# Expert stage of a hybrid attention and mixture-of-experts step: one tile per loop turn, three places for weight blocks, exact tile count

## Chip, core and metric

The kernel runs on one core of a Trainium2 chip. The metric is the device time of one execution in microseconds, as the median of several runs. TensorE (PE), VectorE (DVE), ScalarE (ACT), GpSimd (POOL) and SyncE (SP) each work through a list of their own; they wait for each other through semaphores. DMA transfers are issued by SP and by POOL, each on a queue of its own.

## What is computed

One layer of a backbone on 640 tokens (512 latent, 128 context), width 1024: a combined projection, two kinds of attention, a merge, and then a mixture of experts with 16 experts, of which each token uses two. The change touches only that last part:

```python
def hier_moe(h, w_coarse, b_coarse, w_fine, b_fine, w_gate_up, w_down):
    ...                                    # group of experts, then the top 2 of its 4 experts
    for e in range(N_EXPERTS):             # 16; D = 1024, EXPERT_FF = 512
        gg, uu = jnp.split(t @ w_gate_up[e], 2, axis=-1)
        out = out + combine[:, e:e + 1] * ((jax.nn.silu(gg) * uu) @ w_down[e])
```

All of it is float32. The kernel gets float32 accuracy on TensorE by splitting both operands into a rounded part ("hi") and a rest ("lo") and by making three matmuls, hi·hi, hi·lo and lo·hi.

## The kernel before

The 1280 pairs of token and expert are sorted by expert in memory (`expert_rows`) into tiles of 128 rows. Each expert has one tile, and an expert with more than 128 rows has further tiles. A tile is one matrix of 128 rows by 1024 that is multiplied with the weights of one expert.

Per tile the expert stage does this:

- POOL loads the tile's rows into `expert_in` (line 1848, `load_rows`, 512 KB). `expert_in` has two places, `s` = 0 and 1.
- TensorE transposes them (line 1618, `turn_x`), ACT rounds them (882, `round_x`), DVE takes the rest (1337, `rest_x`).
- SP loads the three weight blocks of the expert, gate, up and down, each 2 MB as four chunks of 512 KB (line 660), alternately into `w_raw` and `w_raw_odd`. ACT rounds each chunk to `w_hi` (878), DVE takes the rest to `w_lo` (1332). There are two places of each; a block reuses the place of the block two before it.
- TensorE makes the gate and the up half of the hidden rows (lines 1632 to 1634, `gate_up`, 48 matmuls). ACT and DVE apply the activation (887, 1344, 1349). TensorE transposes the result (1655, `turn_hidden`), ACT and DVE split it (896, 1353), and TensorE makes the output rows (1647 to 1649, `down`, 24 matmuls).
- ACT copies the output to `expert_out_rows` (892, `take_out`; two places), and POOL stores it back to `expert_rows` (1853, `store_rows`, 512 KB) and waits until it has landed.

The order is written out by hand and software-pipelined by one tile. TensorE's turn for a tile is: `gate_up(tile)`, `turn_x(tile + 1)`, `down(tile - 1)`, `turn_hidden(tile)`. The loop body holds two tiles (`for s in range(2)`), and the number of loop turns comes at run time from `control`, which the routing on DVE has written; `route_done` tells the other engines that it is there. So the stage handles an even number of tiles. POOL's turn for one tile is:

```python
load_rows(2 * i + 3 + s, 1 - s)     # waits x_turned >= tile - 1 + OFF, then the DMA
store_rows(2 * i + s, s, i)         # waits for take_out, DMA, waits until it has landed
```

With `t` as the tile that is stored, the load ahead of it is that of tile `t + 3`. Before the loop POOL has loaded the tiles 0, 1 and 2.

Ahead of the stage SP loads the first gate block into `w_raw` and the first up block into `w_raw_odd`, whose memory is that of the last normalization step; so the second one waits for `yb_done` and for the stores of the normalized rows. The other blocks wait for `route_done`, as which expert they are of is read from `control`. Behind the stage POOL gathers the two output rows of each token (1872), and DVE, ACT and POOL combine and normalize them.

Of the kernel before, what the change touches and what calls it, by code (L numbers as in the profile page):

```python
# [60 lines left out]
TILES = NE + OVER + (NE + OVER) % 2  # L61
# [34 lines left out]
def hybrid_step(nc, t):  # L96

    with ExitStack() as ctx:
# [296 lines left out]
        s4 = ExitStack()  # L395
        ot_hi = [sb("oA_turned_hi", [P, KD, NT * P], F32R, s4)]
# [39 lines left out]
        raw_odd = sb("w_raw_odd", [P, NC_CH, 2, CW], F32, s4)  # L436
# [26 lines left out]
        xs = sb("expert_in", [P, 2, D], F32, s6)  # L463
        xt_hi = sb("expert_in_hi", [P, 2, KD, P], F32R, s6)
        xt_lo = sb("expert_in_lo", [P, 2, KD, P], F32R, s6)
# [4 lines left out]
        yo = sb("expert_out_rows", [P, 2, D], F32, s6)  # L470
# [16 lines left out]
        xs_in = [sem(f"expert_in{i}") for i in range(2)]  # L487
# [4 lines left out]
        raw2_in = [sem(f"w_raw_odd_in{c}") for c in range(NC_CH)]  # L492
# [7 lines left out]
        y_st = [sem(f"expert_out_stored{i}") for i in range(2)]  # L500
# [19 lines left out]
        def landing(q, half, c):  # L520

            if q % 2:
                return raw_odd[:, c], raw2_in[c], 16 * (half + 1)
            return w_raw[:, c], raw_in[c], 16 * (NB + half + 1)
# [5 lines left out]
        def step_blocks(i, s):  # L530

            return [(6 * i + n, n % 2, 3 * i + n // 2) for n in range(3 * s + 2, 3 * s + 5)]
# [7 lines left out]
        def last_pair_of_tiles(eng):  # L540

            return eng.value_load(ctl[0:1, 0:1], min_val=NE // 2 - 1, max_val=TILES // 2 - 1)
# [51 lines left out]
        def _(sp):  # L594
# [61 lines left out]
            def block_in(q, par, half, chunk, r):  # L656
                for c in range(NC_CH):
                    dst, done, _ = landing(par, half, c)
                    sp.wait_ge(lo_done, NC_CH * (NB + q - 2) + c + 1)
                    sp.dma_start(dst, chunk(r, c)).then_inc(done, 16)  # L660

# [10 lines left out]
            def tile_expert(tile):  # L672
                e = sp.value_load(ctl[0:1, bass.ds(1 + tile, 1)], min_val=0, max_val=NE - 1)
                return lambda r, c: expert_chunk(bass.ds(e, 1), r, c).rearrange("p o k n -> p (o k) n")

            sp.wait_ge(route_done, 1)
            last_pair = last_pair_of_tiles(sp)
            with sp.Fori(0, last_pair) as i:
                for s in range(2):
                    chunk = tile_expert(2 * i + 1 + s)  # L680
                    for r, (q, par, half) in enumerate(step_blocks(i, s)):
                        if r == 2:
                            chunk = tile_expert(2 * i + s)
                        block_in(q, par, half, chunk, r)
            chunk = tile_expert(2 * last_pair + 1)
            for r, (q, par, half) in enumerate(step_blocks(last_pair, 0)):
                block_in(q, par, half, tile_expert(2 * last_pair) if r == 2 else chunk, r)
            block_in(6 * last_pair + 5, 1, 3 * last_pair + 2, chunk, 2)
# [20 lines left out]
        def _(act):  # L709
# [159 lines left out]
            act.wait_ge(pj_ready, N_PJ2)  # L869

            def split_hi_moe(block):
                q, par, half = block
                for c in range(NC_CH):
                    src, done, value = landing(par, half, c)
                    act.wait_ge(done, value)
                    if not (isinstance(q, int) and q < 2):
                        act.wait_ge(moe_used, used(q - 2) + c + 1)
                    act.copy(w_hi[:, (NB + par) % 2, c], src).then_inc(hi_done, 1)  # L878

            def round_x(tile, s):  # L880
                act.wait_ge(x_turned, tile + 1 + OFF)
                act.copy(xt_hi[:, s].rearrange("p k q -> p (k q)"), pair[1][:]).then_inc(xh_done, 1)
# [16 lines left out]
            def act_tile(i, s, final):  # L899
                tile, (gate, up, down) = 2 * i + 1 + s, step_blocks(i, s)  # L900
                split_hi_moe(down)
                gate_tanh(tile, gate[0])
                nq = 6 * i + 3 * s + 5
                if final:
                    split_hi_moe((nq, 1, 3 * i + 2))
                else:
                    split_hi_moe((nq, (3 * s + 5) % 2, 3 * i + (3 * s + 5) // 2))
                    round_x(tile + 1, s)
                    split_hi_moe((nq + 1, (3 * s + 6) % 2, 3 * i + (3 * s + 6) // 2))
                take_out(tile - 1, s, down[0])  # L910
                round_hidden(tile)

# [3 lines left out]
            last_pair = last_pair_of_tiles(act)  # L916
            act.wait_ge(y_free, OFF)
            round_x(0, 0)
            split_hi_moe((2, 0, 1))
            gate_tanh(0, 0)  # L920
            split_hi_moe((3, 1, 1))
            round_x(1, 1)
            round_hidden(0)
            with act.Fori(0, last_pair) as i:
                for s in range(2):
                    act_tile(i, s, False)
            act_tile(last_pair, 0, True)
            take_out(2 * last_pair + 1, 1, 6 * last_pair + 5)

# [5 lines left out]
        def _(dve):  # L935
# [373 lines left out]
            for i in range(2):  # L1309
# [4 lines left out]
            link(dve.tensor_tensor(cle[:, 0, 0:MORE // 2], ovc[:, NE - 1:NE].to_broadcast([P, MORE // 2]),  # L1314
                                   tab[:, T_PAIR:T_PAIR + MORE // 2], ALU.is_gt))
            link(dve.tensor_reduce(cf[:, 0:1], cle[:, 0, 0:MORE // 2], AX.X, ALU.add))
            link(dve.tensor_scalar(cf[:, 0:1], cf[:, 0:1], float(NE // 2 - 1), None, ALU.add))
# [10 lines left out]
            def split_lo_moe(block):  # L1328
                q, par, _ = block
                for c in range(NC_CH):  # L1330
                    dve.wait_ge(hi_done, NC_CH * (NB + q) + c + 1)
                    dve.tensor_tensor(w_lo[:, (NB + par) % 2, c], landing(par, 0, c)[0], w_hi[:, (NB + par) % 2, c].bitcast(F32),  # L1332
                                      ALU.subtract).then_inc(lo_done, 1)

            def rest_x(tile, s):
                dve.wait_ge(xh_done, tile + 1 + OFF)
                dve.tensor_tensor(xt_lo[:, s].rearrange("p k q -> p (k q)"), pair[1][:],  # L1337
                                  xt_hi[:, s].rearrange("p k q -> p (k q)").bitcast(F32), ALU.subtract).then_inc(xl_done, 1)
# [18 lines left out]
            def dve_tile(i, s, final):  # L1357
                tile, (gate, up, down) = 2 * i + 1 + s, step_blocks(i, s)
                split_lo_moe(down)
                silu(tile)  # L1360
                nq = 6 * i + 3 * s + 5
                if final:
                    split_lo_moe((nq, 1, 0))
                    times_up(tile, up[0])
                else:
                    split_lo_moe((nq, (3 * s + 5) % 2, 0))
                    times_up(tile, up[0])
                    rest_x(tile + 1, s)
                    split_lo_moe((nq + 1, (3 * s + 6) % 2, 0))
                rest_hidden(tile)  # L1370

            dve.wait_ge(route_done, 1)
            last_pair = last_pair_of_tiles(dve)
            split_lo_moe((0, 0, 0))
            split_lo_moe((1, 1, 0))
            rest_x(0, 0)
            split_lo_moe((2, 0, 0))
            silu(0)
            split_lo_moe((3, 1, 0))
            times_up(0, 1)  # L1380
            rest_x(1, 1)
            rest_hidden(0)
            with dve.Fori(0, last_pair) as i:
                for s in range(2):
                    dve_tile(i, s, False)
            dve_tile(last_pair, 0, True)
# [13 lines left out]
        def _(pe):  # L1400
# [214 lines left out]
            def turn_x(tile, s, landed):  # L1615
                pe.wait_ge(xs_in[s], landed)
                for k in range(KD):
                    last = pe.transpose(pair[1][:, k * P:(k + 1) * P], xs[:, s, k * P:(k + 1) * P], ident[:])
                last.then_inc(x_turned, 1)

            def gate_up(tile, s, blks):
                for r, (q, par, _) in enumerate(blks):
                    if r == 0:
                        pe.wait_ge(xl_done, tile + 1 + OFF)
                        pe.wait_ge(hid_done, tile + OFF)
# [46 lines left out]
            with pe.Fori(0, last_pair) as i:  # L1672
                for s in range(2):
                    pe_tile(i, s, False)
# [269 lines left out]
```

## Time and profile before

| | us |
|---|---|
| median of 3 runs (lowest, highest) | 1662.11 (1661.32, 1665.05) |
| span of the profiled execution | 1662.6 |
| TensorE busy | 1336.0 (80%) |
| TensorE weight load busy | 1087.6 (65%) |
| VectorE busy | 1085.6 (65%) |
| ScalarE busy | 705.8 (42%) |
| GpSimd busy | 250.3 (15%) |
| mean granted TensorE clock | 0.910 |

The whole span falls into projections, attention, merge and normalization, routing (to about 1164 us), the scatter of the rows (to 1190 us), the expert stage (1195 to 1581 us) and the final combination. Shares over the whole span hide that; the expert stage is read by itself, from its own windows.

### The profile page before, as it was taken

The numbers are of one execution on the slowest core, as the hardware profiler recorded it, in microseconds if no ns is written. First come the engines' busy times: TensorE is split into PE (matmuls) and PEld (weight loads), VectorE is DVE, ScalarE is ACT, GpSimd is POOL, SyncE is SP. The second block draws the span as 40 slices with busy tenths as digits, with TensorE's granted clock in tenths as the row PEclk, the third lists the DMA queues.
The fourth block names the chain that finished last, engine by engine and source line by source line (L and its number), as shares of the span: only waits on it lengthen the run. The fifth ranks groups of instructions, "written<-read, shape, count | busy, mean of one in ns | idle before, by whom it ended". The sixth has DMA issues, their size and how long they took to land.

```text
span 1662.6 us, 21046 instructions
## 1 busy us (share of the span) xinstructions
PE 1336.0 (80%) x6852; PEld 1087.6 (65%) x6852; DVE 1085.6 (65%) x1891; ACT 705.8 (42%) x1008; POOL 250.3 (15%) x278
## 2 busy tenths in 40 slices
PE   2599999967999877889995999783299999999800
PEld 0377776655788766788884788563178887777600
DVE  6556552489822377755556634766289999999665
ACT  3523333232322366545444212002078787778600
POOL 0002111011120000000000331453300000000044
PEclk7799999989999999999997999985599999999955
DMA  6545555433473576611203884421889999999642
GB/s 229 167 139 191 193 181 182 147 116 100 146 236 110 151 176 154 180 41 59 73 17 104 298 297 134 166 89 63 316 291 393 392 392 393 392 392 392 258 177 88
DMA packets 152376, 333.05 MB, mean 200 GB/s; under 512 B 17595, under 2 KB 23259, under 8 KB 152299
## 3 DMA queue, kind: packets, MB, share of 16 engines
q1 hardware_dynamic: 123914, 233.22, 41.3%
q0 software_dynamic: 26944, 93.59, 16.1%
q10 hardware_dynamic: 1440, 5.24, 1.0%
q8 instruction: 45, 0.74, 0.2%
q14 instruction: 33, 0.26, 0.1%
HBM read 263.41 MB, written 68.58 MB: 200 GB/s over the span
## 4 chain that ended last, share of the span: by engine, by line
PE 50%; DVE 20%; DMA 13%; issue 9%; ACT 6%; POOL 1%; SPq 0%; ACTq 0%; POOLq 0%; DVEq 0%
PE psum_pair L1425 7%; PE psum_pair L1427 7%; PE psum_pair L1426 7%; DMA w_raw_odd<-in_w_gate_up 4%; DMA w_raw<-in_w_gate_up 4%; PE psum_pair L1518 4%; PE psum_pair L1505 3%; PE psum_pair L1557 3%; PE psum_pair L1558 3%; PE psum_pair L1559 3%; PE psum_pair L1495 3%; DVE w_lo L941 3%; DVE w_lo L1332 2%; ACT p_turned L375 2%; DVE minus_max L1101 2%
## 5 line engine op out<-in xcount | busy, mean ns | idle before, releaser
L941 DVE TENSOR_TENSOR w_lo<-w_raw,w_hi 128x1024 fp32r<-128x1024 f32 x124 | 146.5, 1222 | 152.0 <-ACT w_hi L715 150.2
L1425 PE MATMUL psum_pair<-w_hi,h_hi 128*128 128x512 f32 x520 | 212.3, 408 | 34.7 <-DVE w_lo L941 31.2
L1426 PE MATMUL psum_pair<-w_lo,h_hi 128*128 128x512 f32 x520 | 208.1, 400 | 0.0
L1427 PE MATMUL psum_pair<-w_hi,h_lo 128*128 128x512 f32 x520 | 208.1, 400 | 0.0
L1101 DVE TENSOR_REDUCE minus_max<-psum_pair 128x1 f32<-128x640 f32 (+1 forms) x160 | 114.3, 715 | 96.6 <-PE psum_pair L1495 96.0
L715 ACT CAST w_hi<-w_raw 128x1024 fp32r<-128x1024 f32 x124 | 124.2, 1048 | 120.8 <-DMA w_raw<-in_w_ada 61.5
L799 ACT ACTIVATE p_unnormed<-psum_pair,minus_max 128x640 f32<-128x640 f32 (+1 forms) x160 | 113.4, 709 | 142.2 <-DVE minus_max L1101 142.2
L1332 DVE TENSOR_TENSOR w_lo<-w_raw,w_hi 128x1024 fp32r<-128x1024 f32 x120 | 143.2, 1222 | 22.8 <-ACT w_hi L878 18.6
L1332 DVE TENSOR_TENSOR w_lo<-w_raw_odd,w_hi 128x1024 fp32r<-128x1024 f32 x120 | 143.1, 1221 | 12.0 <-ACT w_hi L878 8.4
L878 ACT CAST w_hi<-w_raw 128x1024 fp32r<-128x1024 f32 x120 | 123.4, 1051 | 45.4 <-DMA w_raw<-in_w_gate_up 26.2
L1425 PEld LDWEIGHTS psum_pair<-w_hi,h_hi 128*128 128x128 f32 x520 | 101.2, 195 | 63.4 <-issue 39.3
L878 ACT CAST w_hi<-w_raw_odd 128x1024 fp32r<-128x1024 f32 x120 | 123.7, 1050 | 35.2 <-DMA w_raw_odd<-in_w_gate_up 25.3
L1632 PE MATMUL psum_pair<-w_hi,expert_in_hi 128*128 128x512 f32 x320 | 129.9, 406 | 7.3 <-DVE expert_in_lo L1337 7.2
L1495 PE MATMUL psum_pair<-k_bundle,q_bundle 128*128 128x512 f32 (+1 forms) x576 | 126.3, 337 | 6.8 <-ACT p_unnormed L799 6.1
L1518 PE MATMUL psum_pair<-v_bundle,p_turned 128*128 128x64 f32 (+1 forms) x1008 | 131.4, 275 | 0.0
L1634 PE MATMUL psum_pair<-w_hi,expert_in_lo 128*128 128x512 f32 x320 | 128.0, 400 | 0.0
L1633 PE MATMUL psum_pair<-w_lo,expert_in_hi 128*128 128x512 f32 x320 | 128.0, 400 | 0.0
L1518 PEld LDWEIGHTS psum_pair<-v_bundle,p_turned 128*128 128x128 f32 x1008 | 122.9, 193 | 1.3
L1427 PEld LDWEIGHTS psum_pair<-w_hi,h_lo 128*128 128x128 f32 x520 | 100.9, 194 | 22.1
L1426 PEld LDWEIGHTS psum_pair<-w_lo,h_hi 128*128 128x128 f32 x520 | 101.4, 195 | 20.4
L1495 PEld LDWEIGHTS psum_pair<-k_bundle,q_bundle 128*128 128x128 f32 x576 | 87.2, 191 | 14.6 <-issue 7.9
L726 ACT ACTIVATE turned_staging<-psum_pair 128x1024 f32<-128x1024 f32 (+1 forms) x38 | 36.3, 957 | 105.2 <-PE psum_pair L1453 105.2
(267 smaller groups left out, 2424.7 us busy)
## 6 DMA issues: line engine op xcount, KB each, us to landing
w_raw<-in_w_gate_up SPq DMA_DIRECT2D x80, 512.0 KB, 8.9
w_raw_odd<-in_w_gate_up SPq DMA_DIRECT2D x80, 512.0 KB, 9.4
w_raw<-in_w_in SPq DMA_DIRECT2D x52, 512.0 KB, 5.2
w_raw<-in_w_ada SPq DMA_DIRECT2D x48, 512.0 KB, 5.4
w_raw<-in_w_down SPq DMA_DIRECT2D x40, 512.0 KB, 9.5
w_raw_odd<-in_w_down SPq DMA_DIRECT2D x40, 512.0 KB, 9.5
expert_rows<-zeros POOLq DMA_DIRECT2D x27, 512.0 KB, 6.0
k_bundle<-k_transposed SPq DMA_DIRECT2D x28, 384.0 KB, 8.7
```

The costliest lines, as they stand in the source:

```text
L878: act.copy(w_hi[:, (NB + par) % 2, c], src).then_inc(hi_done, 1)
L941: dve.tensor_tensor(w_lo[:, b % 2, c], w_raw[:, c], w_hi[:, b % 2, c].bitcast(F32), ALU.subtract).then_inc(lo_done, 1)
L1101: dve.tensor_reduce(nmax[:, m % RR:m % RR + 1], spair(m)[:, 0:width(j)], AX.X, ALU.max, negate=True).then_inc(nb_done, 1)
L1332: dve.tensor_tensor(w_lo[:, (NB + par) % 2, c], landing(par, 0, c)[0], w_hi[:, (NB + par) % 2, c].bitcast(F32), ALU.subtract).then_inc(lo_ ...
L1425: pe.matmul(bank(n), a_hi, hi, start=first, stop=False)
L1426: pe.matmul(bank(n), a_hi, lo, start=False, stop=False)
L1427: last = pe.matmul(bank(n), a_lo, hi, start=False, stop=end)
L1495: last = pe.matmul(spair(m)[:, c0:c0 + w], q, k[:, g, k0:k0 + w], start=g == 0, stop=g == 1)
L1518: last = pe.matmul(obank(j)[:, 0:w], ptb[:, j % 2, k], vb[bi % 2][:, vt, 0:w], start=k == 0, stop=k == len(tiles) - 1)
L1632: pe.matmul(out, xt_hi[:, s, kk], hi, start=kk == 0, stop=False)
L1633: pe.matmul(out, xt_hi[:, s, kk], lo, start=False, stop=False)
L1634: last = pe.matmul(out, xt_lo[:, s, kk], hi, start=False, stop=kk == KD - 1)
```

## The change

The expert stage is rewritten with a loop body of one tile.

- `TILES` is 25 and not 26, and `control[0]` holds the exact number of tiles less two, not a number of pairs. Two small DVE operations ahead of `route_done` go.
- The weight blocks get three places. Raw: `w_raw`, `w_raw_b`, `w_raw_c`. Split: the two places of `w_hi` and `w_lo` and a third, `w_hi_c` and `w_lo_c`. A block waits for the one three before it, on SP and on ACT. The two new raw places share memory with the turned attention rows, which are free after the last matmul of the output projection; SP loads the first up block and the second gate block there as soon as that matmul is done, without waiting for the normalization.
- `expert_in`, its split forms and `expert_out_rows` have one place where they had two. `load_rows` waits for the transposes of the tile just before it; `take_out` waits until the store of the tile before has landed.
- POOL's turn is: load of tile `t + 2`, store of tile `t`. TensorE's order within a tile stays.

```diff
-TILES = NE + OVER + (NE + OVER) % 2
+TILES = NE + OVER
...
-            sp.wait_ge(yb_done, NT)
-            sp.wait_ge(x1_st[0], 16 * 3)
-            sp.wait_ge(x1_st[1], 16 * 2)
             for c in range(NC_CH):
-                sp.dma_start(raw_odd[:, c], expert_chunk(0, 1, c)).then_inc(raw2_in[c], 16)
+                sp.dma_start(raw_b[:, c], expert_chunk(0, 1, c)).then_inc(raw_b_in[c], 16)
+            for c in range(NC_CH):
+                sp.dma_start(raw_c[:, c], expert_chunk(1, 0, c)).then_inc(raw_c_in[c], 16)
...
+                for c in range(NC_CH):
+                    sp.wait_ge(lo_done, NC_CH * (NB + q - 3) + c + 1)
...
-            def take_out(tile, s, q):
+            def take_out(tile, q):
                 act.wait_ge(moe_used, used(q + 1))
-                act.wait_ge(y_free, tile - 1 + OFF)
-                act.copy(yo[:, s], pair[3][:]).then_inc(y_copied, 1)
+                act.wait_ge(y_free, tile + OFF)
+                act.copy(yo[:], pair[3][:]).then_inc(y_copied, 1)
...
-            def load_rows(tile, s):
-                pool.wait_ge(x_turned, tile - 1 + OFF)
-                pool.dma_start(xs[:, s], slot_tiles[bass.ds(tile, 1)]...).then_inc(xs_in[s], 16)
+            def load_rows(tile):
+                pool.wait_ge(x_turned, tile + OFF)
+                pool.dma_start(xs[:], slot_tiles[bass.ds(tile, 1)]...).then_inc(xs_in, 16)
...
-            def store_rows(tile, s, half):
+            def store_rows(tile):
                 pool.wait_ge(y_copied, tile + 1 + OFF)
-                pool.dma_start(slot_tiles[...], yo[:, s]).then_inc(y_st[s], 16)
-                pool.wait_ge(y_st[s], 16 * (half + 1))
+                pool.dma_start(slot_tiles[...], yo[:]).then_inc(y_st, 16)
+                pool.wait_ge(y_st, 16 * (tile + 1))
                 pool.nop().then_inc(y_free, 1)
...
-            load_rows(2, 0)
-            with pool.Fori(0, last_pair) as i:
-                for s in range(2):
-                    load_rows(2 * i + 3 + s, 1 - s)
-                    store_rows(2 * i + s, s, i)
+            pool.wait_ge(x_turned, 1 + OFF)
+            pool.dma_start(xs[:], slot_tiles[1]).then_inc(xs_in, 16)
+            with pool.Fori(0, middle) as i:
+                load_rows(i + 2)
+                store_rows(i)
```

TensorE's loop after the change:

```python
with pe.Fori(0, middle) as i:
    half_of_hidden(i + 1, gate_block(i + 1), 0)
    half_of_hidden(i + 1, up_block(i + 1), 1)
    turn_x(i + 2)
    down(i, down_block(i))
    turn_hidden(i + 1)
```

## Rows read from the trace of the kernel before

**Rows 1.** Stretches of the stage: busy time by engine, PEclk, DMA share, GB/s
```profile
1240.00:1250.00 10.00, 10.00 (x49) 8.24 (x48) 9.32 (x10) 8.39 (x10) 0.70 (x2) 1.00 0.99 354
...
1300.00:1540.00 240.00, 236.36 (x1089) 191.42 (x1089) 219.81 (x206) 189.87 (x205) 13.85 (x26) 1.00 1.05 392
```

**Rows 2.** TensorE in order of time: start us, us, line, what, count
```profile
1230.30 1.03 PE L1618 MATMUL psum_pair<-identity,expert_in 128*128 128x128 f32 x8
...
1236.75 0.60 PE L1655 MATMUL psum_pair<-identity,expert_hidden 128*128 128x128 f32 x4
...
1248.34 1.04 PE L1618 MATMUL psum_pair<-identity,expert_in 128*128 128x128 f32 x8
...
1356.93 1.03 PE L1618 MATMUL psum_pair<-identity,expert_in 128*128 128x128 f32 x8
...
1543.66 1.04 PE L1618 MATMUL psum_pair<-identity,expert_in 128*128 128x128 f32 x8
```

**Rows 3.** Chain of waits within the stage: start us, us, what ended last
```profile
1374.62 10.40 DMA w_raw<-in_w_gate_up
```

**Rows 4.** Instructions on `expert_rows`: count, ns min/median/max, first and last start
```profile
L1853 POOL DMA_DIRECT2D expert_rows<-expert_out_rows x20: 532/537/539, 1239.6 to 1578.4; - x20
```

**Rows 5.** GpSimd in order of time: its stores and loads, idle time and releaser
```profile
1239.63 0.54 POOL L1853 DMA_DIRECT2D expert_rows<-expert_out_rows  x1 [24.44 <-ACT expert_out_rows L892]
1247.72 0.53 POOL L1848 DMA_DIRECT2D expert_in<-expert_rows  x1 [7.55 <-DMA expert_rows<-expert_out_rows]
...
1350.05 0.54 POOL L1853 DMA_DIRECT2D expert_rows<-expert_out_rows  x1 [10.51 <-ACT expert_out_rows L892]
...
1357.50 0.53 POOL L1848 DMA_DIRECT2D expert_in<-expert_rows  x1 [6.91 <-DMA expert_rows<-expert_out_rows]
```

**Rows 6.** ScalarE in order of time: copy of the first tile's output
```profile
1237.90 1.01 ACT L892 COPY expert_out_rows<-psum_pair 128x1024 f32<-128x1024 f32 x1
```

**Rows 7.** TensorE in order of time: last matmul of the stage
```profile
1576.20 0.40 PE L1649 MATMUL psum_pair<-w_hi,hidden_lo 128*128 128x512 f32 x1
```

**Rows 8.** Chain of waits at the end of the stage
```profile
1576.71 1.02 ACT expert_out_rows L892
...
1578.38 2.88 DMA expert_rows<-expert_out_rows
```

**Rows 9.** DMA issues of 1200 to 1540 us: count, KB each, median us to landing
```profile
expert_in<-expert_rows POOLq DMA_DIRECT2D x17, 512.0 KB, 6.6
expert_rows<-expert_out_rows POOLq DMA_DIRECT2D x17, 512.0 KB, 6.6
```

**Rows 10.** DMA issues, 1238 to 1241 us
```profile
w_raw<-in_w_gate_up SPq DMA_DIRECT2D x2, 512.0 KB, 7.0
expert_rows<-expert_out_rows POOLq DMA_DIRECT2D x1, 512.0 KB, 7.3
```

**Rows 11.** SyncE in order of time: weight loads issued, start us, us
```profile
1235.84 3.95 SPq L660 DMA_DIRECT2D w_raw<-in_w_gate_up  x4
1241.77 4.03 SPq L660 DMA_DIRECT2D w_raw_odd<-in_w_gate_up  x4
1247.17 4.22 SPq L660 DMA_DIRECT2D w_raw<-in_w_down  x4
```

**Rows 12.** TensorE in order of time: its one stall inside the stage
```profile
1216.16 0.65 PE L1655 MATMUL psum_pair<-identity,expert_hidden 128*128 128x128 f32 x4 [2.18 <-DVE expert_hidden L1349]
1217.49 0.49 PE L1632 MATMUL psum_pair<-w_hi,expert_in_hi 128*128 128x512 f32 x1 [0.68 <-DVE expert_in_lo L1337]
```

**Rows 13.** Stretches of 1 us after that stall, columns as in the first group
```profile
1218.00:1219.00 1.00, 1.00 (x5) 0.78 (x5) 0.17 (x1) 0.00 (x0) 0.00 (x0) 0.78 1.09 408
1219.00:1220.00 1.00, 1.00 (x4) 0.81 (x3) 0.00 (x0) 0.44 (x1) 0.00 (x0) 0.50 1.03 414
...
1222.00:1223.00 1.00, 1.00 (x6) 0.83 (x5) 0.00 (x0) 0.88 (x1) 0.00 (x0) 1.00 0.08 31
```

**Rows 14.** Stretch of 1 us between the scatter's end and the stage
```profile
1191.00:1192.00 1.00, 0.00 (x0) 0.00 (x0) 0.00 (x0) 0.00 (x0) 1.00 (x3) 0.50 0.07 27
```

More of the change, by code:

```diff
@@ L486, in hybrid_step @@
         scat_st = sem("rows_scattered")
-        xs_in = [sem(f"expert_in{i}") for i in range(2)]
+        xs_in = sem("expert_in")
         x_turned = sem("expert_in_turned")
@@ L514, in hybrid_step, with landing, landed, expert_hi @@
         w_dn = t["w_down"][0].rearrange("e (k p) n -> p e k n", p=P)
[L520 to L524, printed above, removed]
+        def landing(place, c):
+            return ((w_raw, raw_in, NB), (raw_b, raw_b_in, 0), (raw_c, raw_c_in, 0))[place][0][:, c]
+        def landed(place, turn, c):
+            done, earlier = ((raw_in, NB), (raw_b_in, 0), (raw_c_in, 0))[place]
+            return done[c], 16 * (earlier + turn + 1)
+        def expert_hi(place, c):
+            return hi_c[:, c] if place == 2 else w_hi[:, 1 - place, c]
+        def expert_lo(place, c):
+            return lo_c[:, c] if place == 2 else w_lo[:, 1 - place, c]
         def used(q):
             return NC_CH * q + OFF
-        def step_blocks(i, s):
-            return [(6 * i + n, n % 2, 3 * i + n // 2) for n in range(3 * s + 2, 3 * s + 5)]
+        def gate_block(tile):
+            return 3 * tile - 1, 2, tile - 1
+        def up_block(tile):
+            return 3 * tile, 0, tile
+        def down_block(tile):
+            return 3 * tile + 4, 1, tile + 1
+        def last_block(tile):
+            return 3 * tile + 2, 2, tile
         def expert_chunk(e, r, c):
@@ L654, in _ @@
                 load_x(tt)
[L656 to L660, printed above, removed]
             for c in range(NC_CH):
@@ L665, in _, with expert_in @@
             sp.wait_ge(pj_ready, last_no[NB - 1] + 1)
[L666 to L668 removed]
             for c in range(NC_CH):
[L670 to L672 removed]
+                sp.dma_start(raw_b[:, c], expert_chunk(0, 1, c)).then_inc(raw_b_in[c], 16)
+            for c in range(NC_CH):
+                sp.dma_start(raw_c[:, c], expert_chunk(1, 0, c)).then_inc(raw_c_in[c], 16)
+            def expert_in(block, tile, r):
+                q, place, _ = block
                 e = sp.value_load(ctl[0:1, bass.ds(1 + tile, 1)], min_val=0, max_val=NE - 1)
[L674 removed]
+                for c in range(NC_CH):
+                    sp.wait_ge(lo_done, NC_CH * (NB + q - 3) + c + 1)
+                    sp.dma_start(landing(place, c), expert_chunk(bass.ds(e, 1), r, c).rearrange("p o k n -> p (o k) n")).then_inc(
+                        landed(place, 0, c)[0], 16)
             sp.wait_ge(route_done, 1)
[L677 to L688 removed]
+            middle = middle_tiles(sp)
+            with sp.Fori(0, middle) as i:
+                expert_in(up_block(i + 1), i + 1, 1)
+                expert_in(down_block(i), i, 2)
+                expert_in(gate_block(i + 2), i + 2, 0)
+            expert_in(up_block(middle + 1), middle + 1, 1)
+            expert_in(down_block(middle), middle, 2)
+            expert_in(last_block(middle + 1), middle + 1, 2)
             sp.wait_ge(moe_over, 1)
@@ L868, in _, with round_x @@
                 act.nop().then_inc(sm, OFF)
-            act.wait_ge(pj_ready, N_PJ2)
             def split_hi_moe(block):
-                q, par, half = block
+                q, place, turn = block
                 for c in range(NC_CH):
[L874 to L880, printed above, removed]
+                    act.wait_ge(*landed(place, turn, c))
+                    if not (isinstance(q, int) and q < 3):
+                        act.wait_ge(moe_used, used(q - 3) + c + 1)
+                    act.copy(expert_hi(place, c), landing(place, c)).then_inc(hi_done, 1)
+            def round_x(tile):
                 act.wait_ge(x_turned, tile + 1 + OFF)
-                act.copy(xt_hi[:, s].rearrange("p k q -> p (k q)"), pair[1][:]).then_inc(xh_done, 1)
+                act.copy(xt_hi[:].rearrange("p k q -> p (k q)"), pair[1][:]).then_inc(xh_done, 1)
             def gate_tanh(tile, q):
@@ L897, in round_hidden @@
                                scale=0.5).then_inc(ah_done, 1)
[L899 to L911, printed above, removed]
+            act.wait_ge(pj_ready, last_no[NB - 1] + 1)
             split_hi_moe((0, 0, 0))
@@ L1355, in rest_hidden @@
                                          ALU.mult, ALU.subtract).then_inc(al_done, 1)
[L1357 to L1370, printed above, removed]
             dve.wait_ge(route_done, 1)
-            last_pair = last_pair_of_tiles(dve)
+            middle = middle_tiles(dve)
             split_lo_moe((0, 0, 0))
             split_lo_moe((1, 1, 0))
-            rest_x(0, 0)
-            split_lo_moe((2, 0, 0))
+            split_lo_moe(gate_block(1))
+            rest_x(0)
             silu(0)
-            split_lo_moe((3, 1, 0))
+            split_lo_moe(up_block(1))
             times_up(0, 1)
-            rest_x(1, 1)
+            rest_x(1)
             rest_hidden(0)
[L1383 to L1386, printed above, removed]
+            with dve.Fori(0, middle) as i:
+                split_lo_moe(down_block(i))
+                silu(i + 1)
+                split_lo_moe(gate_block(i + 2))
+                times_up(i + 1, up_block(i + 1)[0])
+                rest_x(i + 2)
+                split_lo_moe(up_block(i + 2))
+                rest_hidden(i + 1)
+            split_lo_moe(down_block(middle))
+            silu(middle + 1)
+            split_lo_moe(last_block(middle + 1))
+            times_up(middle + 1, up_block(middle + 1)[0])
+            rest_hidden(middle + 1)
             dve.wait_ge(s7_in, 64)
@@ L1613, in _, with turn_x @@
                 pe.nop().then_inc(sm, OFF)
-            def turn_x(tile, s, landed):
-                pe.wait_ge(xs_in[s], landed)
+            def turn_x(tile):
+                pe.wait_ge(xs_in, 16 * (tile + 1))
                 for k in range(KD):
-                    last = pe.transpose(pair[1][:, k * P:(k + 1) * P], xs[:, s, k * P:(k + 1) * P], ident[:])
+                    last = pe.transpose(pair[1][:, k * P:(k + 1) * P], xs[:, k * P:(k + 1) * P], ident[:])
                 last.then_inc(x_turned, 1)
[L1621 to L1625, printed above, removed]
-                    out = pair[0][:, r * FF:(r + 1) * FF]
-                    for c in range(NC_CH):
-                        pe.wait_ge(lo_done, NC_CH * (NB + q) + c + 1)
-                        for k in range(2):
-                            kk = 2 * c + k
-                            hi, lo = w_hi[:, (NB + par) % 2, c, k], w_lo[:, (NB + par) % 2, c, k]
-                            pe.matmul(out, xt_hi[:, s, kk], hi, start=kk == 0, stop=False)
-                            pe.matmul(out, xt_hi[:, s, kk], lo, start=False, stop=False)
-                            last = pe.matmul(out, xt_lo[:, s, kk], hi, start=False, stop=kk == KD - 1)
-                        last.then_inc(moe_used, 1)
@@ L1637, in down, with half_of_hidden @@
-            def down(tile, blk):
-                q, par, _ = blk
+            def half_of_hidden(tile, block, r):
+                q, place, _ = block
+                if r == 0:
+                    pe.wait_ge(xl_done, tile + 1 + OFF)
+                    pe.wait_ge(hid_done, tile + OFF)
+                out = pair[0][:, r * FF:(r + 1) * FF]
+                for c in range(NC_CH):
+                    pe.wait_ge(lo_done, NC_CH * (NB + q) + c + 1)
+                    for k in range(2):
+                        kk = 2 * c + k
+                        hi, lo = expert_hi(place, c)[:, k], expert_lo(place, c)[:, k]
+                        pe.matmul(out, xt_hi[:, kk], hi, start=kk == 0, stop=False)
+                        pe.matmul(out, xt_hi[:, kk], lo, start=False, stop=False)
+                        last = pe.matmul(out, xt_lo[:, kk], hi, start=False, stop=kk == KD - 1)
+                    last.then_inc(moe_used, 1)
@@ L1639, in down @@
+            def down(tile, block):
+                q, place, _ = block
                 pe.wait_ge(al_done, tile + 1 + OFF)
```

115 lines of the change are left out of this document (59 added, 56 removed).

## Prediction, written before the change was run

> **What bounds the kernel now.** I read the expert stage by itself. First the busy time by stretch: from 1300 to 1540 us all 16 DMA engines are full (share 1.05, 392 GB/s) and TensorE is busy for 236.4 of 240 us [rows 1]. Then TensorE in order of time, where the start of `turn_x` marks a tile. I call that start T. Between 1230.30 and 1356.93 us lie 7 tiles, 18.09 us each; between 1356.93 and 1543.66 lie 10, 18.67 us each [rows 2]. A tile moves twelve weight chunks, one load of rows and one store, 14 x 0.524 MB = 7.34 MB, and 7.34 MB at 392 GB/s takes 18.7 us. TensorE alone takes 6.45 us from T to `turn_hidden` (1230.30 to 1236.75) and 11.6 us from there to the next T (1236.75 to 1248.34), in all 18.0 us. So the stage is first bound by TensorE, later by DMA bandwidth with TensorE 0.6 us behind; the chain of waits shows it as a 10.40 us transfer into `w_raw` [rows 3]. The third thing to read is GpSimd's turn: store, wait until it has landed, load [rows 5]. It is on no path to the end now, since it works one tile further ahead than TensorE needs.
>
> **The change, part by part.**
>
> *Exact tile count.* The output was stored 20 times [rows 4], so 20 tiles ran. That is 16 + 3 or 16 + 4 rounded up. The trace cannot say which; the routing of the given inputs, worked out from the reference, has three experts with more than 128 rows (144, 140 and 191) and the next has 126. So 19 tiles are real, and one tile of 18.7 us goes. The two small DVE operations are worth nothing that can be seen.
>
> *Three places for weights.* Loads and splits run one block further ahead. In the part bound by bandwidth this buys nothing per tile, since the bytes of a tile stay. If nothing else binds, it extends the stretch of 18.1 us tiles by a few.
>
> *One place for rows in and out.* Here a loop closes. TensorE's transposes of tile t + 2 need `load_rows(t + 2)`. That comes on GpSimd behind `store_rows(t - 1)` having landed, which needs `take_out(t - 1)`, which needs `down(t - 1)`, and this stands on TensorE behind the transposes of tile t + 1. Before, the load behind the same store was that of tile t + 3, with a whole tile in hand. Behind the stalled transposes TensorE has queued `down`, `turn_hidden` and the next 48 matmuls, so the stall is the stage's. From T to the next T:
> - T to the end of `down`. `turn_hidden` starts at T + 6.45 [rows 2]; at the end of the stage the copy starts 0.51 us after the last matmul's start [rows 7, 8], and that start is 0.23 us ahead of `turn_hidden`. So the copy can start at T + 6.73. In the trace it starts at T + 7.60 (1237.90) [rows 6], held by splits that wait for a place of `w_hi`; with three places they don't.
> - The copy's start to the store's issue: 1237.90 to 1239.63, 1.73 us [rows 5, 6]. Store issued at T + 8.46.
> - Store issued to load issued: 1239.63 to 1247.72, 8.09 us, later 1350.05 to 1357.50, 7.45 us [rows 5]. I take 7.8.
> - Load issued to landed: median 6.6 us [rows 9]; 0.1 us for the start of the transposes is my estimate.
> Sum 8.46 + 7.8 + 6.6 + 0.1 = 22.9 us, 4.3 us more than the 18.67 of now. The two transfers take 6.6 to 7.3 us beside weight traffic [rows 9, 10] and 2.88 us on empty channels [rows 8]. With a period of 22.9 us the channels would carry 320 GB/s. The stretch 1240 to 1250 had 354 GB/s [rows 1], weight chunks issued from 1235.84, 1241.77 and 1247.17 [rows 11], and its store still took 7.3 us [rows 10] and its load was issued T + 17.4. This is nearly the pattern that I expect: chunks from about T + 5, T + 11 and T + 16. So I take the loaded times; the empty ones (8.46 + 3.8 + 2.9 + 0.1 = 15.3, under 18.67, no stall at all) are the lower end.
>
> What the Trainium skill says speaks against this. "DMA: Bandwidth & Descriptors" (Queues, rings and completion order) has each DMA engine go round-robin between queues, packet by packet. With two queues at work a 512 KB transfer would then get half the rate, by my estimate some 4.3 us, and the loop would take 8.5 + 5.2 + 4.3 + 0.1 = 18.1 us: no stall. The trace disagrees wherever both queues work: 6.6 to 7.3 us.
>
> *The clock.* TensorE idled 2.18 and 0.68 us around 1217 us [rows 12]. After that its granted clock was 0.5, the 1.2 GHz level, and back at 1.0 by 1222 [rows 13]. The 48 matmuls from 1217.49 to T at 1230.30 took 12.8 us, where they otherwise take 11.3: a price of 1.5 us. A stall of 4 us in each tile should bring the same fall, and part of it lies on the loop, on transposes and `down`. Bounds 0 and 1.5 us per tile; I take 0.7, as a later store also meets fewer weight chunks. Period 23.6 us, from the second tile of the loop on.
>
> *Start.* The first up and the second gate block load earlier, and a third block now loads during the scatter. That can leave a backlog when the first rows are loaded, where the channels are now empty (share 0.07 [rows 14]): between 0 and 6.6 - 2.9 = 3.7 us later. I take 1.5, for the scatter uses another queue.
>
> *End.* From T of the last tile (1543.66) to the last store's landing (1578.38 + 2.88 = 1581.26) it is 37.6 us [rows 2, 8]. Weights no longer wait there, but the slow clock costs 1.5: I take 38.5. The part behind the stage stays.
>
> **The sum.** T of the third tile moves from 1230.30 to 1231.8. Sixteen further tiles follow: 22.9 + 15 x 23.6 = 376.9 us, so T of the last tile is 1608.7, and the last store has landed at 1647.2, against 1581.3: 65.9 us more (17 intervals of 18.4 us, 313.4 us, become 16 intervals of 23.6). The profiled span of 1662.6 becomes 1728.5; it lies 0.5 us above the median, so the forecast is 1728 us.
>
> **Rivals.**
> - *The loop of the rows doesn't bind: faster.* If the two transfers together take under 10 us, the period stays at 18.7. They can by finding the channels free (2.88 us each), or by an even share with the weights: 2 x 0.524 MB / 392 GB/s = 2.7 us, with the 1.5 us beyond pure transfer in the 2.88, is 4.2 us each. Then the tile saved decides: T of the last tile 1230.3 + 16 x 18.7 = 1529.5, last store 1567, 14 us less: about 1648 us; with some tiles at 18.1, 1642. It decides below a period of 19.4 us, where 16 intervals fit into 313 us. For it: the idle channels that a slower loop itself makes. The rule of the Trainium skill cited above would bring this case about. Against it: 7.3 us in the least loaded comparable stretch [rows 10]. Chance 0.12.
> - *The loop binds, but mildly.* The slower loop frees the channels for one of the two transfers, 3 to 4 us instead of 6.6, and the period is 20 to 21.5. At 20.5: 1231.8 + 328 + 38.5 = 1598.3, or 17 us more, 1679 us. Slower as well. For it: at 23 us per tile a fifth of the DMA time is idle. Chance 0.15.
> - *The tile isn't saved.* If the chip's routing gave 20 tiles, one further period comes on top: 1728 + 24 = 1752 us. Against it: 126 against 128 rows is exact counting. Chance 0.02.
> - *No change,* within 0.2%, which is about what a measurement of this kernel can tell: the first rival with a period of 19.2 to 19.6. Chance 0.03.
> - The forecast, a period of 21.5 to 25 us: 0.68.
>
> **Range.** The lower end is a period of about 20.5 us, 1679, rounded to 1678. The upper end is all the clock's price and 7.3 us transfers: period 25 and a start 3.7 us later, T of the last tile 1234.0 + 22.9 + 15 x 25 = 1631.9, last store 1670.4, 89 us more: 1751. Left out are the faster cases and half of the tail above. Faster 0.12, same 0.03, slower 0.85.
>
> **What the changed kernel's profile would show.** 19 stores to `expert_rows`; intervals between the first transposes of two tiles of 22 to 25 us; nearly every tile's transposes waiting for the DMA into `expert_in`, 3 to 5 us; under GpSimd the load released by the landing of the store each time; GB/s at 300 to 340 in place of 392 through the stage; a granted clock that falls in most tiles; ScalarE no longer waiting for weight DMAs. I would be wrong if the transfers on GpSimd's queue took 3 to 4 us beside the weights, so that the transposes never waited and the interval stayed under 19 us.

## The result and the profile after

| | before | after |
|---|---|---|
| median, us | 1663.58 (4 runs) | 1738.99 (4 runs, 1731.09 to 1742.6) |
| ratio to before | | 1.0441 (95%: 1.0423 to 1.046) |
| span of the profiled execution | 1662.6 | 1737.0 |
| TensorE busy | 1336.0 (80%) | 1344.3 (77%) |
| mean granted clock | 0.910 | 0.892 |
| first transposes of the third tile / of the last tile | 1230.30 / 1543.66 | 1230.43 / 1616.28 |

The change makes the kernel 4.4% slower. One tile less runs. From the fourth tile's transposes on a tile takes 24.2 us in the mean, where it took 18.1 to 18.7.

One stretch of the expert stage after the change, with columns as in [rows 1]:

```profile
1300.00:1500.00 200.00, 162.32 (x684) 131.62 (x685) 134.80 (x129) 117.03 (x130) 8.56 (x16) 0.90 0.86 304
```

TensorE was busy 236 of 240 us at clock 1.00 with 392 GB/s [rows 1]. Now it is busy 162 of 200 us at clock 0.90, with 304 GB/s. No resource is full. That is the mark of a closed loop of waits.

What TensorE waited for between 1240 and 1620 us (total, times, longest), in full:

```profile
PE psum_pair L1619 <- DMA expert_in<-expert_rows: 68.2, 16, 5.3
```

There is one waiter and one cause: the transposes of the tile's rows (line 1619 now, 1618 before) wait for GpSimd's load, 16 times, 4.3 us each. This row has no counterpart in the same stretch before. The stores are counted here (compare [rows 4]):

```profile
L1852 POOL DMA_DIRECT2D expert_rows<-expert_out_rows x19: 534/539/542, 1238.9 to 1653.1; - x19
```

19 stores, so 19 tiles.

One turn of the loop, first on TensorE and then on GpSimd (start us, us, line; in brackets the idle time before it and what ended it):

```profile
1352.94 1.97 PE L1619 MATMUL psum_pair<-identity,expert_in 128*128 128x128 f32 x8 [3.95 <-DMA expert_in<-expert_rows]
...
1376.75 1.09 PE L1619 MATMUL psum_pair<-identity,expert_in 128*128 128x128 f32 x8 [3.38 <-DMA expert_in<-expert_rows]
```

```profile
1363.67 0.54 POOL L1852 DMA_DIRECT2D expert_rows<-expert_out_rows  x1 [18.28 <-ACT expert_out_rows L906]
1369.39 0.53 POOL L1847 DMA_DIRECT2D expert_in<-expert_rows  x1 [5.19 <-issue]
```

From the transposes at 1352.94 it is 10.7 us to the issue of the store, 5.7 us to the issue of the load, and 7.4 us to the next transposes: 23.8 us. "issue" as releaser of the load means that the profile shows no other wait that ended there; the program has GpSimd wait for the landing of the store at that place. Read from its end, the chain of waits after the change goes from the store's transfer to the load's transfer, tile after tile:

```profile
1238.90 6.74 DMA expert_rows<-expert_out_rows
...
1246.74 6.84 DMA expert_in<-expert_rows
...
1264.50 5.03 DMA expert_rows<-expert_out_rows
...
1270.59 8.04 DMA expert_in<-expert_rows
```

Before, that chain went through the transfers into the weight places [rows 3].

The clock around that turn of the loop, in stretches of 1 us with columns as in [rows 1]:

```profile
1350.00:1351.00 1.00, 0.00 (x0) 0.00 (x0) 0.43 (x1) 0.00 (x0) 0.00 (x0) 0.99 1.04 422
1351.00:1352.00 1.00, 0.00 (x0) 0.00 (x0) 0.00 (x0) 0.00 (x0) 0.00 (x0) 0.50 1.03 406
1352.00:1353.00 1.00, 0.06 (x1) 0.06 (x1) 0.00 (x0) 0.00 (x0) 0.00 (x0) 0.50 1.05 406
...
1356.00:1357.00 1.00, 1.00 (x4) 0.81 (x3) 1.00 (x1) 1.00 (x2) 0.00 (x0) 0.50 0.71 262
...
1358.00:1359.00 1.00, 1.00 (x6) 0.82 (x5) 1.00 (x2) 1.00 (x2) 0.00 (x0) 1.00 0.00 0
```

TensorE stands still from 1349.0 to 1352.9. The granted clock is still near 1.0 in the first part of that stall. It is 0.5 (1.2 GHz) when the rows arrive, and 1.0 again at 1358. So the transposes and part of `down` run at half speed: 1.97 us for the eight transposes, where they took 1.03 [rows 2]. After the stall that ends at 1376.75 they take 1.09 us. The fall doesn't come in every turn at the same place.

### The profile page after: what moved, and what is told of

Its sections match the earlier page's. It is cut to its first block, busy times and chain, and to the rows that moved or that the text cites. A ratio compares the mean times of both kernels' runs of the same rounds, so it can differ in the third digit from the quotient of the medians.

```text
span 1737.0 us, 20890 instructions
## 1 busy us (share of the span) xinstructions
PE 1344.3 (77%) x6768; PEld 1093.8 (63%) x6768; DVE 1061.8 (61%) x1873; ACT 683.0 (39%) x992; POOL 251.4 (14%) x274
## 4 chain that ended last, share of the span: by engine, by line
PE 53%; DVE 16%; DMA 16%; issue 8%; ACT 5%; POOL 2%; POOLq 0%; SPq 0%; ACTq 0%; DVEq 0%
DMA expert_in<-expert_rows 7%; PE psum_pair L1426 6%; PE psum_pair L1428 6%; PE psum_pair L1427 6%; DMA expert_rows<-expert_out_rows 5%; PE psum_pair L1519 3%; PE psum_pair L1506 3%; PE psum_pair L1558 3%; PE psum_pair L1560 3%; PE psum_pair L1559 3%; PE psum_pair L1496 3%; DVE w_lo L951 3%; PE psum_pair L1648 2%; PE psum_pair L1649 2%; PE psum_pair L1650 2%
## 5 line engine op out<-in xcount | busy, mean ns | idle before, releaser
L951 DVE TENSOR_TENSOR w_lo<-w_raw,w_hi 128x1024 fp32r<-128x1024 f32 x124 | 146.5, 1222 | 151.7 <-ACT w_hi L731 150.0
L731 ACT CAST w_hi<-w_raw 128x1024 fp32r<-128x1024 f32 x124 | 124.2, 1047 | 119.9 <-DMA w_raw<-in_w_ada 60.4
L1619 PE MATMUL psum_pair<-identity,expert_in 128*128 128x128 f32 x152 | 30.0, 361 | 111.4 <-DMA expert_in<-expert_rows 111.4
L1619 PEld LDWEIGHTS psum_pair<-identity,expert_in 128*128 128x128 f32 x152 | 23.5, 183 | 118.9 <-DMA expert_in<-expert_rows 118.6
L1344 DVE TENSOR_TENSOR expert_in_lo<-psum_pair,expert_in_hi 128x1024 fp32r<-128x1024 f32 x19 | 23.3, 1225 | 112.7 <-ACT expert_in_hi L896 112.7
L1339 DVE TENSOR_TENSOR w_lo<-w_raw_b,w_hi 128x1024 fp32r<-128x1024 f32 x76 | 88.0, 1220 | 4.2 <-ACT w_hi L892 4.2
L1339 DVE TENSOR_TENSOR w_lo<-w_raw,w_hi 128x1024 fp32r<-128x1024 f32 x76 | 87.8, 1218 | 1.4 <-issue 1.2
L1339 DVE TENSOR_TENSOR w_lo_c<-w_raw_c,w_hi_c 128x1024 fp32r<-128x1024 f32 x76 | 87.9, 1219 | 0.2 <-ACT w_hi_c L892 0.2
L896 ACT CAST expert_in_hi<-psum_pair 128x1024 fp32r<-128x1024 f32 x19 | 19.2, 1013 | 148.7 <-PE psum_pair L1619 148.7
```

Source lines behind the costliest of these rows:

```text
L731: act.copy(w_hi[:, b % 2, c], w_raw[:, c]).then_inc(hi_done, 1)
L951: dve.tensor_tensor(w_lo[:, b % 2, c], w_raw[:, c], w_hi[:, b % 2, c].bitcast(F32), ALU.subtract).then_inc(lo_done, 1)
L1339: dve.tensor_tensor(expert_lo(place, c), landing(place, c), expert_hi(place, c).bitcast(F32), ALU.subtract).then_inc(lo_done, 1)
L1619: last = pe.transpose(pair[1][:, k * P:(k + 1) * P], xs[:, k * P:(k + 1) * P], ident[:])
```

## The experiments

**e1, the load ahead of the store.** The changed kernel, with single places throughout; the wait for the last load is adjusted to one load more.

```diff
+            load_rows(2)
             with pool.Fori(0, middle) as i:
-                load_rows(i + 2)
+                load_rows(i + 3)
                 store_rows(i)
```

> The changed kernel with one thing moved: GpSimd issues the load of tile t + 3 ahead of the store of tile t, and not the load of tile t + 2 behind it; all places stay single. Theory A (the load queued behind the landing of the store closes a loop of 24 us): the transposes never wait, the interval between the first transposes of two tiles falls from 24.2 to between 18.0 and 18.7 us, and with one tile less than before the time is 1638 to 1650 us, under the kernel before. Rival B (the single places of the rows, or the third weight place, cost the time by themselves): it stays over 1690 us.

Measured: 1637.34 us (ratio 0.9841, 0.9817 to 0.9865). From the third tile on the transposes wait for nothing, and the intervals are 17.95 or 17.96 us, the last one 18.54. The stretch 1300 to 1500 us:

```profile
1300.00:1500.00 200.00, 200.00 (x941) 164.51 (x940) 185.28 (x175) 161.15 (x175) 12.30 (x23) 1.00 1.05 392
```

Two neighbouring transfers on GpSimd:

```profile
1355.44 0.53 POOL L1847 DMA_DIRECT2D expert_in<-expert_rows  x1 [10.70 <-PE psum_pair L1619]
1362.16 0.54 POOL L1852 DMA_DIRECT2D expert_rows<-expert_out_rows  x1 [6.19 <-ACT expert_out_rows L906]
```

The load now goes out 1.7 us after the transposes start (1353.74 in that trace), with 16 us in hand for a transfer of 6.6. TensorE is busy for 200 of 200 us. So with the load ahead of the store neither the single places nor the third weight place cost anything; the place of one DMA in GpSimd's program costs 1739 - 1637 = 102 us. Rival B falls.

**e3, the same late load in the kernel before.** Two places of everything, 20 tiles. `load_rows` also waits for the transposes of one tile more, which come earlier on TensorE than the store that the load now stands behind.

```diff
             def load_rows(tile, s):
-                pool.wait_ge(x_turned, tile - 1 + OFF)
+                pool.wait_ge(x_turned, tile + OFF)
...
-            load_rows(2, 0)
             with pool.Fori(0, last_pair) as i:
                 for s in range(2):
-                    load_rows(2 * i + 3 + s, 1 - s)
+                    load_rows(2 * i + 2 + s, s)
                     store_rows(2 * i + s, s, i)
...
-            pool.wait_ge(xs_in[0], 16 * (last_pair + 2))
+            pool.wait_ge(xs_in[0], 16 * (last_pair + 1))
```

> The kernel before, with its two places of everything, where only GpSimd's load is issued one tile later, behind the store of the tile before, as in the change. Theory A: the interval rises from 18.4 to 24 to 25 us, 17 intervals, so 1662 + 17 x 6 = about 1760 us (1745 to 1785). Rival B (single places or the third weight place are the cause): it stays at 1662 us.

Measured: 1802.28 us (ratio 1.083, 1.0795 to 1.0865), slower still than the changed kernel and 17 us above the range that I gave. Theory A holds in kind. The interval is 26.6 us and not 24 to 25. One part of the difference shows on ScalarE, in order of time:

```profile
1361.25 1.01 ACT L882 CAST expert_in_hi<-psum_pair 128x1024 fp32r<-128x1024 f32 x1 [6.87 <-PE psum_pair L1618]
1363.05 1.05 ACT L878 CAST w_hi<-w_raw_odd 128x1024 fp32r<-128x1024 f32 x1 [0.78 <-PE psum_pair L1649]
1364.44 1.05 ACT L878 CAST w_hi<-w_raw_odd 128x1024 fp32r<-128x1024 f32 x1 [0.35 <-PE psum_pair L1649]
...
1368.19 1.00 ACT L892 COPY expert_out_rows<-psum_pair 128x1024 f32<-128x1024 f32 x1
```

With two places of `w_hi` each split waits for a chunk of `down` (line 1649), so the copy comes 8.95 us after the transposes (1359.24 there). The size of this wait can be read from the first turn of the loop, in which the transposes still run at full clock: the store goes out 9.32 us after them, in the changed kernel 8.47. So the wait is worth some 0.85 us. I had left it, which I had seen in [rows 6], out of my expectation. The rest is the clock and the transfers. In the later turns, nearly all with transposes of 1.97 us after stalls of 4.8 to 7.0 us, the store goes out after 10.6 to 12.2 us, in the mean 11.6. It then takes 8.08 us to the issue of the load, against 6.39 in the same turns of the changed kernel, and the load 6.90 against 7.52.

**e4, the load behind the store's issue, ahead of its landing.** The changed kernel; `store_rows` no longer contains the wait for the landing.

```diff
+            load_rows(2)
             with pool.Fori(0, middle) as i:
-                load_rows(i + 2)
                 store_rows(i)
+                load_rows(i + 3)
+                stored(i)          # wait for the landing, then y_free
```

> The changed kernel, where GpSimd issues the load right behind the issue of the store and waits for the store's landing only after that. Theory A: the store's landing (6.3 us) leaves the loop; first transposes to store issue 8.5 us, issue of the load 0.6, load beside a store 7 to 9 us: 16 to 18.5 us, under the 18.7 of the DMA bandwidth, so 1640 to 1655 us. If two transfers side by side on GpSimd's queue take 10 us each, the interval is 19.5 and the time about 1662. Rival B: over 1690 us.

Measured: 1641.92 us (0.9866, 0.9823 to 0.9909), the median of only two runs, 1637.62 and 1646.21; the trace is of the faster one. In it the intervals are 17.95 us for most of the stage and 18.7 to 19.5 at its end. TensorE's waits between 1240 and 1540 us, in full, all in the last four tiles:

```profile
PE psum_pair L1619 <- DMA expert_in<-expert_rows: 3.1, 4, 1.3
```

With the landing of the store out of the loop, almost nothing of the stall is left. The two transfers side by side took 6.5 and 7.8 us (medians), not 10.

**e5, no idle TensorE.** The changed kernel with matmuls in the stall.

```diff
+            def fill(tile):
+                pe.wait_ge(y_copied, tile + OFF)
+                for _ in range(16):
+                    pe.matmul(pair[3][:, 0:CW], xt_hi[:, 0], xt_hi[:, 0:4].rearrange("p k q -> p (k q)"), start=True, stop=True)
...
+                fill(i)
                 turn_x(i + 2)
```

> The changed kernel with 16 extra matmuls (3.7 us at full clock, their result is overwritten) ahead of the transposes of each tile, where TensorE otherwise stands still. If the slow clock after the stall costs 1.5 to 1.9 us per tile on the loop, the interval falls from 24.2 to 22.3 to 23.3 us and the time to 1710 to 1728 us; the store then meets more weight traffic, which gives part of it back. If the clock isn't on the loop, the time stays at 1739 us or rises a little.

Measured: 1727.89 us (1.0383, 1.035 to 1.0415), 11 us less than the changed kernel, at the upper edge of what I expected. It does 16 matmuls more per tile and is faster. The stretch 1300 to 1500 us, where the changed kernel has a granted clock of 0.90:

```profile
1300.00:1500.00 200.00, 187.47 (x863) 151.82 (x862) 142.74 (x136) 124.86 (x138) 9.10 (x17) 1.00 0.87 314
```

TensorE and GpSimd in order of time:

```profile
1349.51 1.09 PE L1619 MATMUL psum_pair<-identity,expert_in 128*128 128x128 f32 x8 [1.41 <-DMA expert_in<-expert_rows]
...
1367.50 3.80 PE L1625 MATMUL psum_pair<-expert_in_hi 128*128 128x512 f32 x16
1372.56 1.09 PE L1619 MATMUL psum_pair<-identity,expert_in 128*128 128x128 f32 x8 [1.26 <-DMA expert_in<-expert_rows]
```

```profile
1357.98 0.54 POOL L1858 DMA_DIRECT2D expert_rows<-expert_out_rows  x1 [14.65 <-ACT expert_out_rows L906]
1365.80 0.53 POOL L1853 DMA_DIRECT2D expert_in<-expert_rows  x1 [7.28 <-issue]
```

The means of the three legs over 16 tiles, worked from such rows (us):

| | transposes to store issued | store issued to load issued | load issued to transposes | sum |
|---|---|---|---|---|
| forecast, clock left out | 8.46 | 7.8 | 6.7 | 22.9 (22.96 before rounding) |
| e5, stall filled | 8.48 | 7.96 | 6.83 | 23.3 |
| changed kernel | 10.15 | 6.48 | 7.48 | 24.1 |

The slow clock costs 1.67 us on the first leg and the store gives back 1.48; the load takes 0.65 more. The net is 0.85 us per tile. The changed kernel's own trace agrees: in its two turns in which the clock stays at 1.00 (transposes at 1230.43 and 1376.75) the legs are those of e5, 8.47, 7.84 and 6.89 us, and 8.48, 8.00 and 6.70. A store that goes out later meets less other traffic: in the turn at 1352.94 all transfers together move 314 GB/s while it is under way (1363.7 to 1369.3), in the turn at 1376.75 it is 346 (1385.3 to 1393.2), and in e5 354 (1358.0 to 1365.7).

**e7, half the bytes of the weights.** The changed kernel; each weight chunk loaded behind `route_done` brings only half its contents, so part of the weights is left out.

```diff
-  sp.dma_start(landing(place, c), expert_chunk(...).rearrange("p o k n -> p (o k) n"))
+  sp.dma_start(landing(place, c)[:, 0:1], expert_chunk(...).rearrange("p o k n -> p (o k) n")[:, 0:1])
```

> The changed kernel, where each weight chunk inside the loop and behind it loads only half its bytes (256 KB); the other half keeps old contents, so part of the input is left out. If the weight traffic is what makes the store and the load on GpSimd's queue slow, they fall from 5.6 and 7.4 us towards 2.9 us, and the interval from 24.1 to 18 to 21 us (1640 to 1685 us). If they are slow by themselves (descriptors, memory), the interval stays at 24 and the time at 1739 us.

Measured: 1658.81 us, a single run, so without an interval. The transfers on GpSimd's queue took (count, KB, median us to landing, 1240 to 1540 us):

```profile
expert_in<-expert_rows POOLq DMA_DIRECT2D x16, 512.0 KB, 5.6
expert_rows<-expert_out_rows POOLq DMA_DIRECT2D x15, 512.0 KB, 4.3
```

In the changed kernel the medians are 7.4 and 5.3 us in the same stretch. The stretches in which a load is under way, in e7 and then in e5:

```profile
1355.80:1361.40 5.60, 4.26 (x19) 3.09 (x17) 5.60 (x6) 3.15 (x4) 0.53 (x1) 1.00 0.87 279
```

```profile
1388.90:1395.70 6.80, 5.49 (x24) 4.14 (x23) 3.29 (x4) 0.75 (x1) 0.50 (x1) 1.00 1.04 397
```

The legs are 8.57, 5.22 and 5.71 us, in sum 19.5. So the weight traffic is what makes these transfers slow, and even half of it doesn't bring them near the 2.88 us of [rows 8].

**e2, one tile more.** e1 with 20 tiles, the last of them on empty rows.

```diff
-TILES = NE + OVER
+TILES = NE + OVER + 1
...
-  link(dve.tensor_scalar(cf[:, 0:1], ovc[:, NE - 1:NE], float(NE - 2), None, ALU.add))
+  link(dve.tensor_scalar(cf[:, 0:1], ovc[:, NE - 1:NE], float(NE - 1), None, ALU.add))
```

> The kernel with the load ahead of the store (one tile period 17.95 us throughout), made to run one tile more than there are, 20 as the kernel before. If a tile that is saved is worth one period of the stage, the time rises by 18.0 to 19 us, from 1637 to 1655 to 1656 us. If the tile count never mattered (the last tile hidden beside something else), it stays at 1637.

Measured: 1658.48 us (0.9971, 0.9959 to 0.9982), 21.1 us more than e1; expected were 18 to 19. Its last four intervals are 18.08, 18.74, 18.71 and 18.71 us where e1 has 17.95 nearly to its end, and its stage began 2.7 us later (first transposes at 1197.85 against 1195.11). Between the kernels the start of the stage lies anywhere from 1191.3 to 1197.9 us, so the 21.1 aren't all the tile's. From the first to the last transposes it is 340.7 us here and 320.8 in e1, 19.9 more. So a tile saved is worth 18.7 to 20 us. (The kernel before took 1663.83 us beside e1 and 1663.95 beside e2 and e6, so they can be compared.)

**e6, weight loads one block later.** e1 with

```diff
-  sp.wait_ge(lo_done, NC_CH * (NB + q - 3) + c + 1)
+  sp.wait_ge(lo_done, NC_CH * (NB + q - 2) + c + 1)
```

> The kernel with the load ahead of the store, where SyncE waits for the block two before and not three before, so that weights load one block later; the three places stay. If the third place is what keeps TensorE fed in the last ten tiles, the interval returns to 18.7 us there, as in the kernel before: about 9 x 0.7 = 6 us more, 1643 us (1641 to 1648). If the third place brings nothing beyond the other splits, it stays at 1637.

Measured: 1641.94 us (0.9868, 0.9852 to 0.9884), 4.6 us more than e1. Its first seven intervals from the third tile on are 17.95 us, then come one of 18.33 and eight of 18.75 to 18.80. That is the pattern of the kernel before. What TensorE waited for between 1228 and 1540 us begins with

```profile
PE psum_pair L1633 <- DVE expert_in_lo L1344: 5.1, 9, 0.7
```

where e1 has one such wait of 0.3 us. So loading one block further ahead is worth some 5 us here: 4.6 in the times, whose intervals overlap a little (e1 reaches to 0.9865, e6 down to 0.9852), and 6.3 in the traces, from the third to the last transposes. It is a lead that is used up and no gain per tile: 7.34 MB in 17.95 us would be 409 GB/s, and e1 moves 392. In e2, one tile longer, the lead ends and the last three intervals are 18.7.

## Why the prediction was right, step by step

The forecast was 1728 us; measured were 1739. Against the span of 1737.0 the sum of 1728.5 is 8.5 us short.

- **What bounded it before**: DMA bandwidth late in the stage, TensorE early. Borne out by e6 and e1: 18.8 us where the loads are late, 17.95 where they are not.
- **The tile count**: 19 stores, as worked out from the reference's routing. The rival of 20 tiles falls. It was taken at 18.7 us; e2 has 19.9 in its trace.
- **The loop through GpSimd**: right, in its mechanism. e3 brings the slowdown into the kernel before by that edit alone, e1 takes it away from the kernel after, and e4 shows that it takes the store's landing and the load in series. Without the clock the legs were forecast at 22.9 us and came to 23.3 in e5.
- **The copy's time**, T + 6.73 with three places: in e5 it starts at T + 6.77 (1356.28) and the store leaves at T + 8.48, forecast 8.46.
- **The period**: 24.18 us (1253.63 to 1616.28 over 15 intervals) where I had 23.6: 15 x 0.58 = 8.7 us, as much as the whole miss. Two terms share it. The legs without the clock were 23.25 us in e5 over these 15 intervals, 0.35 more than the 22.9 that I summed: 0.16 up to the load's issue, 0.12 in the load, and most of the rest from rounding 22.96 down. And the clock, taken at 0.7 net of what the store gives back, costs 24.18 - 23.25, some 0.92, which is 0.22 more.
- **The clock**: right in kind and nearly in net, but the 0.7 was an estimate between bounds, and its parts are larger than I had them. The first leg alone loses 1.67 us, more than the 1.5 of the one stall in the trace of before [rows 12, 13], which I had as the upper bound. Whether it is more because the stalls are longer (4.3 us in the mean) is not shown: behind the longest stall of the changed kernel, 5.30 us, the store went out after 9.81 us, and behind one of 3.49 us after 10.98. What keeps the net small is that the store gives back 1.48, which I had named as a reason for 0.7 but not worked out.
- **The transfers** on GpSimd's queue beside weights: taken at 6.6 to 7.3 us. In the changed kernel the two legs that hold them take 14.0 us together where 14.5 were forecast, with the store quicker and the load slower than I had them; that the two errors cancel is luck. The rule of the Trainium skill in "DMA: Bandwidth & Descriptors" (Queues, rings and completion order), round-robin between the queues by packets, would have made the loop fit into 18.7 us if taken as an even share of the bandwidth. The measured 6.7 to 6.9 us of e5 contradict that use of it: 0.524 MB in 6.8 us is 77 GB/s, a fifth of the 397 that all transfers together moved meanwhile. The even share falls as a rival. Why GpSimd's transfer gets so little is open.
- **Start**: I took 1.5 us later. The first transposes were 2.7 us later, but the second and third tile lie only 14.8 us apart, not 17.4, so the third tile's were 0.1 us later than before. With three places that interval is 14.8 us in e1, e2, e4, e6 and the changed kernel (16.4 in e7, and 18.4 in e5 with its extra matmuls); with two (e3) it is 17.4. Before, TensorE stood still for 2.18 and 0.68 us there and then ran at clock 0.5 [rows 12, 13]; in the changed kernel it stands still for 0.42 and 1.49 us and the clock stays at 1.00. I had not counted this gain. The start itself differs between kernels with the same code ahead of it: 1194.6 and 1191.3 us in the kernel before and e3, 1192.4 to 1197.9 in the others. So the 2.7 us can't be put down to the change.
- **End**: 38.5 us forecast from the last transposes to the last store's landing; it took 39.7, 1616.28 to 1656.0:

```profile
1653.11 2.89 DMA expert_rows<-expert_out_rows
```

The terms add up: third tile 1.4 us earlier than forecast, first interval 23.2 for 22.9, fifteen at 24.18 for 23.6, end 1.2 more: -1.4 + 0.3 + 8.7 + 1.2 = 8.8 us.

The mild case (period 20 to 21.5) needed a transfer of 3 to 4 us beside the weights; not even half the weight traffic gives that (e7).

What stays open is why the load takes 7.48 us in the changed kernel and 6.83 in e5. It goes with how long the store before it took. In the three turns of the changed kernel in which the store took 7.8 us or more, the load took 6.7 to 6.9, as in e5; in the other thirteen the store took 5.5 to 7.3 and the load 7.2 to 8.4. I have no run that separates the two.

## What to carry to other kernels

Giving up a second buffer is judged by the order of the queue that refills the one that is left. Follow each refill back to what stands ahead of it in its engine's program. Here a load that needed only the transposes stood behind the landing of an unrelated store, and moving it ahead of the store turned 4.4% slower into 1.6% faster with the same memory. In a loop of waits take DMA times from a stretch in which the other queues are as busy as they will be, not from empty channels. A stall on such a loop can also bring the slow clock back, as those of 3.4 to 5.3 us did here in most turns, and the first work after it, which is the loop's own, pays.

## What the runs showed of the hardware

- A 512 KB transfer on GpSimd's queue took 2.9 us on empty channels, 4.3 (store) and 5.6 (load) beside half the weight bytes (e7, 267 to 283 GB/s in all while it was under way) and 6.6 to 6.9 beside all of them (e1, e5; 354 to 397 GB/s). The time goes with the traffic at that moment and not with the mean of the stage: e5 has a mean of 314 GB/s and e1 of 392, but while a load is under way both are at 391 to 397, and it takes 6.6 and 6.7 us.
- Sixteen more matmuls per tile made the kernel 11 us faster, because they kept the clock up through a stall: the transposes after it took 1.09 us in all turns but the last (1.58), and not up to 1.97, and the mean granted clock between 1300 and 1500 us was 1.00 and not 0.90.
- With stalls of 0.9 to 1.9 us in nearly every tile (e7) the mean granted clock between 1300 and 1500 us was 0.99, with 3.4 to 5.3 us (changed kernel) 0.90, and with 5.8 to 6.4 us (e3) 0.87.
